# A two-block transformer kernel: the scores of its second attention with the keys on the rows

## The reference, cut to what matters

```python
s = (einsum('bqhd,bkhd->bhqk', qn_b, kn_all)
     + einsum('bqhr,bkr->bhqk', qr_b, kr_all)) * scale
p = softmax(s, axis=-1)
o = einsum('bhqk,bkhd->bqhd', p, v_all)
y = (o * silu(g)) @ w_o
```

## Time and profile before

| | |
|---|---|
| runs shown, us | 2364.46, 2364.59, 2369.76 (median 2364.59) |
| the profiled execution's own time, its span | 2363.17 us, 2361.4 us |
| busy share of the span | PE 92%, PEld 71%, DVE 45%, ACT 36%, POOL 29% |
| mean granted TensorE clock | 0.956 of full speed |
| stage B, first value product to the start of the output products | 607.9 to 859.4 us |

### The profile page before, as it was taken

How to read it: one execution, slowest core, us unless ns; L and a number is a source line. 1 busy time by engine, 2 the same in 40 slices (tenths; PEclk the granted TensorE clock), 3 DMA queues, 4 the chain that set the end, 5 groups by cost and what they waited for, 6 DMA issues and landing times. The chain is left out here.

```text
span 2361.4 us, 29756 instructions
## 1 busy us (share of the span) xinstructions
PE 2183.5 (92%) x11442; PEld 1677.8 (71%) x11442; DVE 1072.2 (45%) x1782; ACT 842.9 (36%) x1563; POOL 689.8 (29%) x383
## 2 busy tenths in 40 slices
PE   5999888899999998997898999998998788999997
PEld 3888555688555544885876888886985566788886
DVE  2421888523355523636616625243117724725253
ACT  3322655323444423335123323223116633322231
POOL 1221000243000002330142444444443343444443
PEclk8999999899999999998689999998999899999999
DMA  7221332132000012320022333322231122333332
GB/s 267 63 63 54 92 97 82 45 108 63 18 1 1 1 36 72 90 81 1 28 63 58 104 101 89 104 82 80 90 89 32 32 65 69 99 97 91 98 94 67
DMA packets 255889, 169.16 MB, mean 72 GB/s; under 512 B 5776, under 2 KB 247159, under 8 KB 254599
## 3 DMA queue, kind: packets, MB, share of 16 engines
q1 hardware_dynamic: 251792, 157.31, 22.4%
q0 software_dynamic: 2336, 8.97, 1.2%
q10 hardware_dynamic: 1623, 0.98, 0.1%
HBM read 165.10 MB, written 2.14 MB: 71 GB/s over the span
## 5 line engine op out<-in xcount | busy, mean ns | idle before, releaser
L1260 POOL TENSOR_TENSOR WL<-raww,WH 128x1024 fp32r<-128x1024 f32 (+1 forms) x239 | 564.7, 2368 | 982.7 <-ACT WH L309 865.6
L354 PE MATMUL ps<-HH,WH 128*128 128x512 f32 (+1 forms) x1368 | 526.2, 385 | 37.2 <-DVE HL L475 19.6
L355 PE MATMUL ps<-HL,WH 128*128 128x512 f32 (+1 forms) x1368 | 521.8, 381 | 0.0
L356 PE MATMUL ps<-HH,WL 128*128 128x512 f32 (+1 forms) x1368 | 520.9, 381 | 0.0
L309 ACT ACTIVATE WH<-raww 128x1024 fp32r<-128x1024 f32 (+1 forms) x239 | 244.9, 1034 | 328.4 <-PE ps L356 328.3
L354 PEld LDWEIGHTS ps<-HH,WH 128*128 128x128 f32 x1368 | 261.7, 191 | 97.8 <-issue 24.5
L356 PEld LDWEIGHTS ps<-HH,WL 128*128 128x128 f32 x1368 | 261.1, 191 | 49.5
L355 PEld LDWEIGHTS ps<-HL,WH 128*128 128x128 f32 x1368 | 261.4, 191 | 47.1
L557 ACT ACTIVATE PB<-ps,NB 128x256 f32<-128x256 f32 (+5 forms) x256 | 167.9, 656 | 101.3 <-DVE NB L546 64.1
L604 PE MATMUL ps<-ident,PB 128*128 128x128 f32 x952 | 156.7, 281 | 23.1 <-DVE PT L622 16.1
L542 DVE TENSOR_REDUCE NB<-ps 128x1 f32<-128x768 f32 (+4 forms) x128 | 92.5, 723 | 128.5 <-PE ps L532 127.5
(11 more groups left out here) (296 smaller groups left out, 3318.3 us busy)
## 6 DMA issues: line engine op xcount, KB each, us to landing
raww<-in_ffn_w_up SPq DMA_DIRECT2D x88, 512.0 KB, 3.8
raww<-in_ada_w SPq DMA_DIRECT2D x32, 512.0 KB, 3.6
raww<-in_ffn_w_down SPq DMA_DIRECT2D x32, 448.0 KB, 3.7
raww<-in_odd_w_in SPq DMA_DIRECT2D x24, 512.0 KB, 3.7
raww<-in_even_w_in SPq DMA_DIRECT2D x21, 512.0 KB, 3.8
raww<-in_a_w_in SPq DMA_DIRECT2D x20, 512.0 KB, 3.8
raww<-in_ffn_w_down SPq DMA_DIRECT2D x16, 512.0 KB, 3.8
ADA<-in_ada_w SPq DMA_DIRECT2D x6, 1024.0 KB, 18.0
```

What stands on the lines that cost most here:

```text
L354: nc.tensor.matmul(out, lh, rh, start=start and k == ks[0], stop=False)
L355: nc.tensor.matmul(out, lh, rl, start=False, stop=False)
L356: ins = nc.tensor.matmul(out, ll, rh, start=False, stop=stop and k == ks[-1])
L1260: nc.gpsimd.tensor_tensor(lo, raw_slot(k), hi.bitcast(F32), ALU.subtract).then_inc(*split_lo.mark(k))
```

## The change

Stage B leaves the generic routines and gets a queue of its own on each engine. For head h:

- `b_rows` multiplies the high parts alone (queries on the rows, 512 + 256 keys, banks 0 and 1) for each of four query tiles; `b_max` (DVE) reduces them. These scores serve the maximum only.
- `b_shift` turns the four columns of negated maxima into a row of 512 with matmuls against the identity, into row 96 of bank 0; `b_shift_act` copies it to row 96 of the query's high part. Row 96 of the key's high part holds ones, so that the product adds the negated maximum.
- `b_cols_low` and `b_cols_high` make the scores of 128 keys x 512 queries in three F32R products (two low, one high with 97 rows), six blocks in turn through banks 2 and 3. `b_exp` writes the exponentials straight to `BT`, which `b_pv` reads.
- POOL adds the six blocks (`b_acc`), `b_sums` multiplies by ones to have the sums of all keys, `b_recip` (DVE) takes the reciprocal of all 512 columns from bank 1 to `BC`, POOL multiplies the gate, `b_keep` the output.
- Keys and queries are made for two heads at once over all 128 columns (`b_keys_up`, `b_queries_up`: banks 4, 5, 6), the rotated queries for four heads at once (`b_rope_up`, bank 1, at head 1, 5, 9). ACT copies the high parts of the next head (`b_keys_act`: 512 and 256 columns, `b_queries_act`, `b_turned_act`: 512 each), DVE makes the low parts (`b_keys_low`, `b_queries_low` from PSUM, `b_turned_low` a copy of 32 rows). The rotation runs once for four heads.
- Ahead of the flow the first up-products stand before the value products, the row products of head 0 between them. The weights `b_w_uq_1` and `b_w_ukv_1` are reordered in the inputs.

The diff, cut to its core:

```diff
-        BQ = over("BQ", KC * R + 6 * S, 4 * S)[:, :].rearrange("p (b r) -> p b r", r=S)
+        BT0 = over("BT0", 0, 6 * S)[:, :].rearrange("p (b q) -> p b q", q=S)
...
-        b_k = part(12032, 1536).rearrange("p (b r) -> p b r", r=R)
+        b_kr = part(12032, 768)
+        b_acc = part(12032, 1536).rearrange("p (b r) -> p b r", r=S)
...
+        BT = [BT0, PT[2], PT[0], PT[1]]
...
+        def b_rows(pe, h, i):
+            q = b_qh[0:96, h % 2, i * P:(i + 1) * P]
+            if i == 0:
+                pe.wait_ge(*act_out["bqr", h])
+            for b in (0, 1):
+                claim(pe, b, (max_made, ("B", h, i)))
+            nc.tensor.matmul(ps[:, 0, :], q, b_kh[0:96, h % 2, 0:S], start=True, stop=True)
+            nc.tensor.matmul(ps[:, 1, 0:C], q, b_kh[0:96, h % 2, S:R], start=True, stop=True)\
+                .then_inc(*scores_made.mark("B rows", h, i))
+        def b_shift(pe, h):
+            claim(pe, 0, (act_out, ("shift", h)))
+            pe.wait_ge(*max_made["B", h, 3])
+            for i in range(NT):
+                ins = nc.tensor.matmul(ps[96:P, 0, i * P:(i + 1) * P], NB[:, h % 4, i:i + 1].to_broadcast([P, 32]),
+                                       ident[:, :], start=True, stop=True)
+            ins.then_inc(*spread_made.mark("shift", h))
+        def b_cols_low(pe, h, kb):
+            c = slice(kb * P, (kb + 1) * P)
+            b = 2 + kb % 2
+            if kb == 0:
+                pe.wait_ge(*dve_out["bqrl", h])
+            claim(pe, b, (exp_made, ("B", h, kb)))
+            nc.tensor.matmul(ps[:, b, :], b_kh[0:96, h % 2, c], b_ql[0:96, h % 2, :], start=True, stop=False)
+            nc.tensor.matmul(ps[:, b, :], b_kl[0:96, h % 2, c], b_qh[0:96, h % 2, :], start=False, stop=False)
+        def b_cols_high(pe, h, kb):
+            if kb == 0:
+                pe.wait_ge(*act_out["shift", h])
+            nc.tensor.matmul(ps[:, 2 + kb % 2, :], b_kh[0:97, h % 2, kb * P:(kb + 1) * P], b_qh[0:97, h % 2, :],
+                             start=False, stop=True).then_inc(*scores_made.mark("B", h, kb))
+        def b_pv(pe, r, q):
+            if q == 0:
+                claim(pe, 7, (o_made, ("B", (r // 2, "lat"))))
+            pe.wait_ge(*exp_made["B", r, q])
+            for h in (r - 1, r):
+                p0 = HD * (h % 2)
+                ins = nc.tensor.matmul(ps[p0:p0 + HD, 7, :], b_v[:, q, h * HD:(h + 1) * HD], BT[h % 4][:, q, :],
+                                       start=(q == 0), stop=(q == 5), skip_group_check=True)
+            if q == 5:
+                ins.then_inc(*pv_made.mark("B", r))
+        def b_sums(pe, r):
+            claim(pe, 1, (rcp_made, ("B", r)))
+            for h in (r - 1, r):
+                p0 = HD * (h % 2)
+                pe.wait_ge(*summed["B", h, 5])
+                ins = nc.tensor.matmul(ps[p0:p0 + HD, 1, :], ones[:, 0:HD], b_acc[:, h % 3, :], start=True, stop=True)
+            ins.then_inc(*spread_made.mark("B", r))
+        b_pv_at, b_sum_at, b_keep_at = {}, {}, {}
+        for r in range(1, 13, 2):
+            b_pv_at.update({(r + 1, 3): [(r, 0)], (r + 1, 4): [(r, 1)], (r + 2, 0): [(r, 2)], (r + 2, 1): [(r, 3)]})
+            b_sum_at[r + 2, 1] = r
+            b_keep_at[r + 3, 0] = r
+        b_pv_at.update({(14, 1): [(13, 0)], (14, 2): [(13, 1)], (14, 3): [(13, 2)], (14, 4): [(13, 3)]})
+        b_sum_at[14, 4], b_keep_at[15, 1] = 13, 13
+        b_pv_at.update({(15, q + 2): [(15, q)] for q in range(4)})
+        def b_flow_pe(pe):
+            for h in range(16):
+                for kb in range(6):
+                    if kb == 0:
+                        b_cols_low(pe, h, 0)
+                        b_cols_low(pe, h, 1)
+                    elif kb > 1:
+                        b_cols_low(pe, h, kb)
+                    b_cols_high(pe, h, kb)
+                    for r, q in b_pv_at.get((h, kb), []):
+                        b_pv(pe, r, q)
+                    if (h, kb) in b_sum_at:
+                        b_sums(pe, b_sum_at[h, kb])
+                    if h < 15 and kb >= 2:
+                        b_rows(pe, h + 1, kb - 2)
+                if h % 2 == 0 and h < 14:
+                    b_keys_up(pe, h // 2 + 1)
+                elif 2 < h < 15:
+                    b_pv(pe, (h - 1) | 1 if h == 14 else h - 2, 4)
+                if h < 15:
+                    b_shift(pe, h + 1)
+                if h % 2 == 0 and h < 14:
+                    b_queries_up(pe, h // 2 + 1)
+                elif 2 < h < 15:
+                    b_pv(pe, (h - 1) | 1 if h == 14 else h - 2, 5)
+                if h % 4 == 1 and h < 13:
+                    b_rope_up(pe, h // 4 + 1)
+            for q in (4, 5):
+                b_pv(pe, 15, q)
+            b_sums(pe, 15)
...
+        def b_shift_act(act, h):
+            act.wait_ge(*spread_made["shift", h])
+            nc.scalar.activation(b_qh[96:97, h % 2, :], ps[96:97, 0, :], ACT.Copy).then_inc(*act_out.mark("shift", h))
+        def b_exp(act, h, kb):
+            act.wait_ge(*scores_made["B", h, kb])
+            if h >= 4 and kb == 0:
+                act.wait_ge(*pv_made["B", (h - 4) | 1])
+            nc.scalar.activation(BT[h % 4][:, kb, :], ps[:, 2 + kb % 2, :], ACT.Exp).then_inc(*exp_made.mark("B", h, kb))
+        def b_flow_act(act):
+            for h in range(16):
+                for kb in range(6):
+                    b_exp(act, h, kb)
+                    if kb == 0 and h < 15:
+                        b_keys_act(act, h + 1)
+                    if kb == 1 and h < 15:
+                        b_queries_act(act, h + 1)
+                        b_turned_act(act, h + 1)
+                if h < 15:
+                    b_shift_act(act, h + 1)
+                if h % 4 == 1 and h < 13:
+                    b_raw_act(act, h // 4 + 1)
+                if h % 4 == 2 and h < 14:
+                    b_rope_high(act, h // 4 + 1)
...
+        def b_max(dve, h, i):
+            dve.wait_ge(*scores_made["B rows", h, i])
+            nc.vector.tensor_reduce(NB[:, h % 4, i:i + 1], ps[:, 0:2, :].rearrange("p a b -> p (a b)")[:, 0:R], AX_X,
+                                    ALU.max, negate=True).then_inc(*max_made.mark("B", h, i))
+        def b_recip(dve, r):
+            dve.wait_ge(*spread_made["B", r])
+            if r >= 3:
+                dve.wait_ge(*gated["B", r - 2])
+            nc.vector.reciprocal(BC, ps[:, 1, :]).then_inc(*rcp_made.mark("B", r))
+        def b_keep(dve, r):
+            g = b_gate(r // 2)
+            dve.wait_ge(*pv_made["B", r])
             dve.wait_ge(*gated["B", r])
...
+            nc.vector.tensor_tensor(g, ps[:, 7, :], g, ALU.mult).then_inc(*o_made.mark("B", (r // 2, "lat")))
...
+        def b_flow_dve(dve):
+            for h in range(16):
+                if h % 4 == 3 and h < 15:
+                    b_rope_low(dve, h // 4 + 1)
+                for kb in range(6):
+                    if (h, kb) in b_keep_at:
+                        b_keep(dve, b_keep_at[h, kb])
+                    if h < 15:
+                        if kb < 2:
+                            b_keys_low(dve, h + 1, kb)
+                        if kb == 1:
+                            b_queries_low(dve, h + 1)
+                            b_turned_low(dve, h + 1)
+                    if (h, kb) in b_sum_at:
+                        b_recip(dve, b_sum_at[h, kb])
+                    if h < 15 and kb >= 2:
+                        b_max(dve, h + 1, kb - 2)
+                    if h % 4 == 2 and h < 14 and kb == 3:
+                        rope_products(dve, ("br", h // 4 + 1), raw[1], ROPE[:, 0, :], ROPE[:, 1, :], S, swap8)
+                    if h % 4 == 2 and h < 14 and kb == 5:
+                        rope_sum(dve, ("br", h // 4 + 1), [(raw[1], 0, P)], S)
+            b_recip(dve, 15)
+            b_keep(dve, 15)
+        def b_gate_pool(pool, r):
+            g = b_gate(r // 2)
+            pool.wait_ge(*rcp_made["B", r])
+            nc.gpsimd.tensor_tensor(g, g, BC, ALU.mult).then_inc(*gated.mark("B", r))
+            pool.wait_ge(*gated["B", r])
+        def b_flow_pool(pool):
+            for h in range(16):
+                if h >= 3:
+                    pool.wait_ge(*spread_made["B", (h - 3) | 1])
+                for kb in range(1, 6):
+                    pool.wait_ge(*exp_made["B", h, kb])
+                    nc.gpsimd.tensor_tensor(b_acc[:, h % 3, :], BT[h % 4][:, 0, :] if kb == 1 else b_acc[:, h % 3, :],
+                                            BT[h % 4][:, kb, :], ALU.add).then_inc(*summed.mark("B", h, kb))
+                    pool.wait_ge(*summed["B", h, kb])
+                    if kb == 1 and h % 2 and h >= 3:
+                        if h < 15:
+                            b_gate_pool(pool, h - 2)
+                if h >= 14:
+                    b_gate_pool(pool, (13, 15)[h - 14])
...
+            pe.wait_ge(*dve_out["cqn", 1])
+            b_rope_up(pe, 0)
+            b_keys_up(pe, 0)
+            b_queries_up(pe, 0)
             for t in range(6):
```

(57 more changed lines are left out.)

157 lines of the change are left out of this document (83 added, 74 removed).

## The result

The changed kernel takes 2431.15 us (median of 4 runs, 2428.10 to 2432.53), the kernel before 2364.53 (4 runs). The ratio is 1.0278 with a 95% interval of 1.0262 to 1.0294: slower by 66.6 us, where 38.4 were forecast. The direction was right, the size was not, and the time lies just outside the range. The profiled execution took 2428.10 us with a span of 2426.3; its mean granted clock fell from 0.956 to 0.936.

A forecast was written before the change was run, and what follows sets the result against it. TensorE was taken to bound stage B, so added waits are paid in full: 28.8 (walk) + 4.0 (DVE behind POOL) + 5.6 (clock) = 38.4 us on 2363.2, so 2402 us; range 2362 to 2430.

The forecast's parts named there:

- walk of the queues, with the reciprocal: Stage B: TensorE's work plus added waits, walked through four queues, 287.2 us against 258.4, so 28.8 us more.
- DVE behind POOL: Stage B: `b_turned_low` and the rotation wait behind POOL's additions, 0.3 us each, 4.0 us; bounds 0 and 10.
- clock: Stage B: half clock after each of 7 reciprocal waits, two rounds growing by 0.4 us: 5.6 us; bounds 0 and 29.
- the clock stays low: Rival: half speed through the rest of 7 heads after long waits, 29.4 us in place of 5.6, 2425 us; chance 0.14.
- Waits: Stage B, TensorE idle: reciprocal 29.2 us, maxima 26.9, rotated queries 13.0, third block 7.1, end 0.7.
- The reciprocal: Stage B: 512 columns take 4.24 us on DVE; TensorE waits ahead of `b_rows` in seven heads, 29.2 us.
- The rotated queries: Stage B, even heads: `b_turned_act` ends late, TensorE is ready for `b_rows` 1.6 us earlier: 13.0 us.
- The maximum: Stage B: one pair of banks for four tiles, TensorE waits for DVE's maximum after row products: 26.9 us.
- TensorE's work: First value product to end of first output product: 210.3 us after the change, 258.4 before; row-score pairs at 0.347 us.
- Covered work: Stage B: ACT under 7 us of a head's 15, POOL's additions 7 us a head, both covered.
- the tests that the prediction set itself: Wrong if the wide reciprocal takes under 2 us, TensorE's stage B share stays above nine tenths, or stage under 258 us.
- the 48 us of saved work: Stage B: without the 381 transposes and plain scores, TensorE's work alone falls by 48 us.

The follow-up runs named there:

- kernel 3: The changed kernel with spare F32R products in TensorE's waits for reciprocals, maxima and rotated queries, head 14's ahead of its row product: 2400.91 us, ratio 1.0159.
- kernel 6: kernel 3 with four of POOL's five additions in each head cut to 8 columns, sums left out: 2396.47 us, ratio 1.0140.
- kernels 8 and 9: 8: split reciprocal plus row scores in two halves with a maximum each, copies and PV moved, 2373.89 us; 9: 8 with the rotation spread behind maxima, 2359.14 us.
- Kernels 7 to 10: 7: changed kernel, reciprocal in four SBUF pieces, PV spread, 2407.18 us; 8: halved row scores, 2373.89; 9: rotation spread, 2359.14; 10: 9 plus spare products, heads 0-1, 2351.42.

## Why the prediction was right or wrong

The direction was forecast rightly, the mechanism in part. Of the 66.6 us the profiled executions hold 64.9: 70.6 us in the stage, less 5.8 given back behind it. The terms, of which the second is only what is left over:

| | forecast | by the runs |
|---|---|---|
| walk of the queues, with the reciprocal | 28.8 | 22.6 with the reciprocal's measured 3.36 us |
| what the walk lacked at full clock | none | 12.1 (kernel 3's 37.7 less 22.6 and 3.0), the spare products' own cost included |
| DVE behind POOL | 4.0 | 3.0 (kernel 6) |
| clock | 5.6 | at least 32.9 (kernel 3) |
| given back behind the stage | none | -5.8 |

- **The failed step is the clock.** The prediction took it as seven long waits with two slow rounds each, 5.6 us, and its own upper bound, the head slow to its end, was 29. The runs show two things in its place, 112.6 us at half clock and 32.9 us of time for it. The clock fell also where no wait was as long as the reciprocal's: at 632.9 us, among waits of 1.1, 0.8 and 1.8 us, and heads 0 to 2 hold 30.7 of the 112.6 us. And behind a reciprocal it stayed low for longer than two rounds: 10.2 us behind six of the seven (728.50 to 738.70 in head 5), half of the head. The bound from the earlier trace rows was read as one event after one idle time. The trace of before held a better row, which the prediction didn't use: the later attention stage, busy 180.69 of 209.59 us, at a clock of 0.80. The changed stage was busy 254.44 of 302.10 us and stood at 0.81. The share of TensorE in the walk (210 of 287 us, 0.73) was a warning too; the prediction gives a like one (0.7 of a head) for its rival "the clock stays low" (2425), which came nearest. That rival's 29.4 us of clock are near the 32.9, in part by luck: it put them all behind the seven long waits. The Trainium skill, "TensorE: Matmul & The Clock Gate" (A second HAM failure mode: psum-queue depth-cycling), says that a kernel that idles briefly between groups of matmuls while it cycles through PSUM banks swings between the two levels. The stage's 0.81 with two banks for four row tiles agrees.
- **Waits: right in kind, not in size.** All three stood where forecast, ahead of the row products. The reciprocal was mis-sized: 3.36 us for 4.24, 7 x 0.88 = 6.2 us less (in the page of waits 21.7 for 29.2). The rotated queries were right (14.4 for 13.0). The maximum comes third and not second: 5.7 us, and 2.3 ahead of the shift rows, for 26.9. A part of it is hidden, as shown in head 5, so its true size at full clock stays open. 6.3 ns for each element lies inside the slopes of the earlier trace rows, 6.0 to 10.5; the lowest one, between 4 and 8 elements of the same line, was the good one. The Trainium skill, "VectorE: DVE Perf Modes" (First, the fixed hardware budget), states a repeat count of 8, from which the prediction estimated 4.27 us; the measured 3.36 differs and decides.
- **TensorE's work was too low.** At full clock kernel 3's stage is 37.7 us over before; the corrected walk (22.6) and POOL's part (3.0) give 25.6, so 12.1 are missing. The rows of kernel 3 point to the change between kinds of product: a pair of row products 0.42 for 0.347 (64 times, 4.7 us), and a PV group between F32R products about 0.2 more than its own time. This is read from distances and wasn't tried by itself; part of the 12.1 us is the spare products' own. Their cause stays open.
- **POOL as a hidden cost: right in kind.** 3.0 against 4.0, all of it in the rotation and none in `b_turned_low`. In kernels 8 and 9 the rotation's place between two maxima that TensorE waits for, together with its stretch, was worth 3 to 5 us in a head.
- **Covered work: right.** ACT and POOL had time to spare, though ACT's order of copies made the wait for the rotated queries; POOL was busy 111 us in the window, as forecast.
- **Luck.** The reciprocal taken too long (6.2 us) and the time given back behind the stage (5.8) together cancel the 12.1 us that the walk lacked. That is chance. The miss that is left in the profiled executions, 26.5 us (64.9 for 38.4), is by size that of the clock, 27.3.

Of the tests that the prediction set itself, the reciprocal is above 2 us, TensorE's share is 254.4/302.1 = 0.84, the stage is longer than 258 us. So none would have told that the sum was wrong, and none of them looked at the clock outside the long waits.

Where did the 48 us of saved work go? With the 70.6 us more there are 118.7 to account for: 70.7 are the walk's waits with the reciprocal as measured (76.9 - 6.2), 32.9 the clock, 3.0 POOL's, 12.1 unexplained. Kernels 7 to 10 take it back by the same road: shorten what TensorE waits for, then see the clock return.

## What to carry to other kernels

If a change takes work from the engine that bounds a stage and puts waits into it, price the clock over the whole stage, with all its waits, and not behind the longest ones alone; if another stage of the trace has TensorE idle about as often, its clock is a first estimate (here 0.80 there and 0.81 in the changed stage). The quickest test of that price is to fill the gaps with spare products: a kernel that becomes faster with more work was held by its clock. A wide DVE reciprocal (3.36 us for 128x512) and operations with two SBUF operands beside a busy POOL belong where nobody waits for the bank or the next maximum, cut in pieces if need be.

## What the runs showed of the hardware

- Wide reciprocal on DVE: 3357 ns for 128x512 from PSUM, 3353 from SBUF, 944 for 128x128: about 6.3 ns for each element, where a copy of 512 takes 0.69 us.
- TensorE's clock fell to half (0.50 from 632.9 to 643.1 us) among waits of 1.1, 0.8 and 1.8 us. Spare products in the waits kept it at 1.00 over 271 us (kernel 3), and the stage was 32.9 us shorter with them.
- The same 1076 matmul instructions of an unchanged stage took 209.6 and 205.2 us in two kernels, at a clock of 0.80 and 0.82. Stage B, behind work that no edit touched, began at 605.8 to 613.8 us in the profiled executions.
- DVE operations of 512 columns with two SBUF operands took 0.67 us alone and up to 1.79 us beside POOL's additions of 1.27 (kernels 8 and 9); a maximum over PSUM in the same stretch took 0.54 to 0.56 us and wasn't stretched.
